# The second block's input projection on x times its weights, with the norm's factor applied at evacuation

## The reference

```
x = x + gate * (p @ ple_proj)            # end of block 1, gate = sigmoid(x @ ple_gate)
x = rms_norm(x, final_g)                 # factor 1 and gain final_g
a = rmsnorm(x, norm_pre_mix_2)           # factor 2 and gain norm_pre_mix_2
proj = a @ w_in_2                        # q,k | v | o gate | gates | c_q | c_kv | k_r
```

## Time and profile before

| | |
|---|---|
| median of 3 runs | 1454.25 us (1454.07 to 1454.81) |
| profiled execution | 1455.51 us, its span 1453.7 us |
| TensorE busy | 1367.2 us, 94% |
| DVE, ACT, POOL busy | 45%, 36%, 36% |
| mean granted TensorE clock | 0.967 |

### The profile page before, as it was taken

The page is one execution under the profiler, slowest core; times in us unless marked ns, Lnnn a source line. Parts: engine busy times, 40 slices in busy tenths (PEclk is TensorE's granted clock), DMA queues, the critical chain, the costliest instruction groups (busy, mean ns, idle before and its releaser), DMA issues.

```text
span 1453.7 us, 15764 instructions
## 1 busy us (share of the span) xinstructions
PE 1367.2 (94%) x6273; PEld 1087.5 (75%) x6273; DVE 652.8 (45%) x856; ACT 521.7 (36%) x794; POOL 519.0 (36%) x229
## 2 busy tenths in 40 slices
PE   4899989999999999999997999889979999999997
PEld 3677889868888888888884875556648888888885
DVE  6547866345422621121365624556465532514223
ACT  4567211254322221221343444444444322313232
POOL 2233250133444444444541432211214444444440
PEclk7899999999999999999998999999989999999998
DMA  5222210122333333332331322100113333333321
GB/s 167 59 61 70 58 30 15 44 73 87 109 96 93 101 98 92 100 99 84 107 96 35 87 66 51 44 29 30 44 44 87 94 95 102 98 91 101 99 75 58
DMA packets 211360, 111.66 MB, mean 77 GB/s; under 512 B 16140, under 2 KB 209496, under 8 KB 211288
## 3 DMA queue, kind: packets, MB, share of 16 engines
q1 hardware_dynamic: 210488, 109.81, 26.5%
q10 hardware_dynamic: 672, 0.79, 0.2%
q0 software_dynamic: 128, 0.07, 0.0%
HBM read 108.55 MB, written 2.10 MB: 76 GB/s over the span
## 4 chain that ended last, share of the span: by engine, by line
PE 86%; DVE 9%; ACT 3%; issue 1%; POOL 1%; DMA 0%; DVEq 0%; ACTq 0%; SPq 0%
PE bank L1711 22%; PE bank L1713 22%; PE bank L1712 21%; PE aux L1886 2%; PE aux L1899 1%; PE bank L1734 1%; PE aux L1061 1%; PE bank L1735 1%; PE bank L1736 1%; PE aux L1896 1%; PE bank L1046 1%; DVE al L2246 1%; DVE rstd L2254 1%; PE aux L975 1%; PE aux L987 1%
## 5 line engine op out<-in xcount | busy, mean ns | idle before, releaser
L1673 POOL TENSOR_TENSOR wl<-raw,wh 128x1024 fp32r<-128x1024 f32 (+1 forms) x202 | 496.6, 2460 | 870.8 <-ACT wh L1990 870.5
L1711 PE MATMUL bank<-ah,wh 128*128 128x512 f32 x984 | 391.7, 398 | 0.1
L1713 PE MATMUL bank<-al,wh 128*128 128x512 f32 x984 | 384.5, 391 | 0.0
L1712 PE MATMUL bank<-ah,wl 128*128 128x512 f32 x984 | 384.5, 391 | 0.0
L1990 ACT CAST wh<-raw 128x1024 fp32r<-128x1024 f32 (+1 forms) x202 | 209.2, 1039 | 352.5 <-PE bank L1713 338.2
L1711 PEld LDWEIGHTS bank<-ah,wh 128*128 128x128 f32 x984 | 185.6, 189 | 43.6 <-issue 5.5
L1712 PEld LDWEIGHTS bank<-ah,wl 128*128 128x128 f32 x984 | 185.7, 189 | 38.9 <-issue 1.4
L1713 PEld LDWEIGHTS bank<-al,wh 128*128 128x128 f32 x984 | 185.5, 188 | 39.1
L1711 PE MATMUL bank<-yh,wh 128*128 128x512 f32 x432 | 168.7, 391 | 0.0
L1713 PE MATMUL bank<-yl,wh 128*128 128x512 f32 x432 | 168.2, 389 | 0.0
L1712 PE MATMUL bank<-yh,wl 128*128 128x512 f32 x432 | 168.1, 389 | 0.0
(11 more groups left out here) (385 smaller groups left out, 1689.3 us busy)
## 6 DMA issues: line engine op xcount, KB each, us to landing
raw<-in_w_up SPq DMA_DIRECT2D x54, 512.0 KB, 4.0
raw<-in_w_down SPq DMA_DIRECT2D x48, 512.0 KB, 4.1
raw<-in_w_in SPq DMA_DIRECT2D x40, 512.0 KB, 3.9
raw<-in_w_gate SPq DMA_DIRECT2D x22, 512.0 KB, 3.8
raw<-in_w_out SPq DMA_DIRECT2D x16, 512.0 KB, 3.7
raw<-in_ple_gate SPq DMA_DIRECT2D x8, 512.0 KB, 4.0
raw<-in_w_down SPq DMA_DIRECT2D x8, 384.0 KB, 3.4
xtok<-in_x SPq DMA_DIRECT2D x4, 512.0 KB, 5.3
```

The costliest lines, as they stand in the source:

```text
L1673: nc.gpsimd.tensor_tensor(wl[b % SPLIT][:, 0:w], raw[b % RAW][:, 0:w], wh[b % SPLIT][:, 0:w].bitcast(F32), ALU.subtract).then_inc(wl_ready, 1)
L1711: nc.tensor.matmul(ps, h[:, c:c + P], mh[:, k, :], start=(n == 0), stop=False)
L1712: nc.tensor.matmul(ps, l[:, c:c + P], mh[:, k, :], start=False, stop=False)
L1713: last = nc.tensor.matmul(ps, h[:, c:c + P], ml[:, k, :], start=False, stop=(n == nk - 1))
```

## The change

- `pgate` reads `yh[1]`, `yl[1]` (free at that time) in place of `ah`, `al`; the splitting of x goes there.
- While the `pgate` tiles run, ACT fills `ah` with x · gains and DVE (`scaled_low`) fills `al`, for each k as soon as x k is final. `gains` is now computed before the loop.
- The last `pgate` tile is done whole. The sums over channels stand inside the pair `gates2`, `qk2` 0: `first_sums` behind k = 1, `last_sums` behind k = 5.
- The factor is kept as a row, `nrow` (the same 512 numbers on all partitions), and, for `v2`, where tokens lie on the partitions, as columns `ncol`, which four tiny products with one partition of `nrow` make after `qk2` 2.
- Every tile of the projection is multiplied by it when it is read. DVE becomes the reader of `qk2`, `o2`, `cq2` and `ckv2`; ACT then works from SBUF. `v2` stays with ACT, with `ncol` as scale.

The core of the diff:

```diff
-                  gate="act", up="dve", down="dve", proj="act", pgate="act", gates2="dve", qk2="act", v2="act",
-                  cq2="act", ckv2="act", o2="act", uq2="dve", uk2="act", uv2="dve", wouta="dve",
+                  gate="act", up="dve", down="dve", proj="act", pgate="act", gates2="dve", qk2="dve", v2="act",
+                  cq2="dve", ckv2="dve", o2="dve", uq2="dve", uk2="act", uv2="dve", wouta="dve",
...
-                    gemm("pgate", m, ready=(al_ready, KD * F_PLE) if m == 0 else None)
-            gemm("pgate", KD - 1, part=(0, 2))
-            ssq(2, early=True)
...
-            gemm("pgate", KD - 1, part=(1, 2))
-            ssq(2)
...
+                    gemm("pgate", m, mov=(yh[1], yl[1]), ready=(al_ready, KD * F_PLE) if m == 0 else None)
+            gemm("pgate", KD - 1, mov=(yh[1], yl[1]))
+            gemm_pair(("gates2", 0), ("qk2", 0), (al_ready, KD * F_NORM3), between={1: first_sums, 5: last_sums})
...
+                if k == 0:
+                    act.wait_ge(gains_ready, 1)
+                    act.wait_ge(gemm_done, LAST_USE[F_NORM2])
+                    act.wait_ge(al_ready, KD * F_NORM3)
+                nc.scalar.activation(ah[:, k, :], x[:, k, :], ACT.Copy, scale=gains[:, k:k + 1]).then_inc(ah_ready, 1)
...
-            link(nc.scalar.activation(sq[:, 0, :], sq[:, 0, :], ACT.Ln, bias=eps2[:, 0:1], scale=1.0 / D))
-            nc.scalar.activation(sq[:, 0, :], sq[:, 0, :], ACT.Exp, scale=-0.5).then_inc(rstd_ready, 1)
-            for k in range(KD):
-                upper(F_NORM3, k, k, h32[:, k % 3, :], (h32_ready, H32_BASE[F_NORM3] + k + 1))
+            link(nc.scalar.activation(nrow[:, :], sq[:, 0, :], ACT.Ln, bias=eps2[:, 0:1], scale=1.0 / D))
+            nc.scalar.activation(nrow[:, :], nrow[:, :], ACT.Exp, scale=-0.5).then_inc(rstd_ready, 1)
...
+            def scaled_low(k):
+                dve.wait_ge(ah_ready, KD * F_NORM3 + k + 1)
+                nc.vector.scalar_tensor_tensor(al[:, k, :], x[:, k, :], gains[:, k:k + 1], ah[:, k, :].bitcast(F32),
+                                               ALU.mult, ALU.subtract).then_inc(al_ready, 1)
...
+                if m > 0:
+                    scaled_low(m - 1)
             dve.wait_ge(x_gated, KD)
+            scaled_low(KD - 1)
...
-            for k in range(KD):
-                dve.wait_ge(al_ready, KD * F_NORM3 + max(0, k - 2))
-                nc.vector.scalar_tensor_tensor(h32[:, k % 3, :], x[:, k, :], gains[:, k:k + 1], both, ALU.mult,
-                                               ALU.mult).then_inc(h32_ready, 1)
-                if k > 0:
-                    lower(F_NORM3, k - 1, k - 1, h32[:, (k - 1) % 3, :])
...
             gemm("qk2", 1)
             gemm("qk2", 2)
+            pe.wait_ge(rstd_ready, 4)
+            for c in range(NC):
+                last = nc.tensor.matmul(aux[3][:, c:c + 1], nrow[0:1, c * P:(c + 1) * P], ones[0:1, 0:1], start=True,
+                                        stop=True)
+            last.then_inc(ncol_ps, 1)
             pe.wait_ge(forget_sums_ready, 1)
...
-                nc.scalar.copy(craw2[j % 2][:, 3:3 + T], bank[t % NBANK][:, :])
-                tile("qk2", j, lambda ps: nc.scalar.activation(cc2[j % 2][:, :], ps, ACT.Copy,
-                                                               scale=g_of("conv_w_2", 12 + j)))
+                tile("qk2", j)
+                evacuated(act, "qk2", j)
+                nc.scalar.activation(cc2[j % 2][:, :], craw2[j % 2][:, 3:3 + T], ACT.Copy,
+                                     scale=g_of("conv_w_2", 12 + j)).then_inc(last_tap, 1)
...
-                    tile("o2", j, lambda ps: nc.scalar.activation(o, ps, ACT.Exp, scale=-1.0))
+                    tile("o2", j)
                     evacuated(act, "o2", j)
+                    link(nc.scalar.activation(o, o, ACT.Exp, scale=-1.0))
...
+            def scaled_qk(j):
+                ps = tile("qk2", j)
+                if j >= 2:
+                    dve.wait_ge(conv2_done, j - 1)
+                    dve.wait_ge(last_tap, j - 1)
+                freed(nc.vector.tensor_tensor(craw2[j % 2][:, 3:3 + T], ps, nrow[:, :], ALU.mult))
...
+            dve.wait_ge(ncol_ps, 1)
+            nc.vector.tensor_copy(ncol[:, :], aux[3][:, 0:NC]).then_inc(ncol_ready, 1)
+            scaled_qk(1)
             conv(0)
+            scaled_qk(2)
             dve.wait_ge(cb_ps, 1)
...
+                elif kind == "proj2":
+                    if i == "o2":
+                        freed(nc.vector.tensor_tensor(og[:, s, :], tile("o2", s), nrow[:, :], ALU.mult))
+                    else:
+                        freed(nc.vector.tensor_tensor(cq[:, s if i == "cq2" else 2, :], tile(i, s), nrow[:, :], ALU.mult))
...
+                    if n in between:
+                        between[n]()
```

More of the change, by code:

```diff
@@ L247, in build @@
         rcol = sb("rcol", [P, NC])
+        ncol = sb("ncol", [P, NC])
         gains = sb("gains", [P, KD])
@@ L362, in build @@
         cq = sb("cq", [P, 3, T], at=offs["vt2"])
+        nrow = sb("nrow", [P, T], at=offs["vt2"] + 4 * 3 * T)
         pm = sb("pm", [P, 3, T], at=offs["trig"])
@@ L560, in build @@
         out_ready = signal("out_ready")
+        gains_ready = signal("gains_ready")
+        ncol_ps = signal("ncol_ps")
+        last_tap = signal("last_tap")
+        ncol_ready = signal("ncol_ready")
+        g2_scaled = signal("g2_scaled")
         SPLIT_AT = [2 * NC * (t + 1) + 1 for t in range(3)]
@@ L1178, in scalar_second @@
                 for c in range(NC):
-                    tile("v2", (pair, c), lambda ps: nc.scalar.copy(v2[:, c, pair * 256:(pair + 1) * 256],
-                                                                    ps[:, 0:256]))
+                    act.wait_ge(ncol_ready, 1)
+                    tile("v2", (pair, c), lambda ps: nc.scalar.activation(v2[:, c, pair * 256:(pair + 1) * 256],
+                                                                          ps[:, 0:256], ACT.Copy,
+                                                                          scale=ncol[:, c:c + 1]))
                     if pair == 1 and c == 0:
@@ L1214, in proj @@
                 else:
-                    tile(kind, j, lambda ps: nc.scalar.copy(cq[:, j if kind == "cq2" else 2, :], ps))
+                    tile(kind, j)
             def keys(j):
@@ L1419, in vector_second @@
             conv(2)
+            scaled_qk(3)
             conv(3)
@@ L1715, in gemm, with gemm_pair @@
                     last.then_inc(gemm_done, 1)
-            def gemm_pair(first, second, ready, order=None):
+            def gemm_pair(first, second, ready, order=None, between={}):
                 t = state["t"]
@@ L2035, in upper @@
                 act.wait_ge(*wait)
-                nc.scalar.copy(ah[:, k, :], src).then_inc(ah_ready, 1)
+                nc.scalar.copy((yh[1] if fill == F_PLE else ah)[:, k, :], src).then_inc(ah_ready, 1)
             tables(LN_EXP_TABLES)
```

52 lines of the change are left out of this document (29 added, 23 removed).

## The result

The changed kernel takes **1441.32 us** (median of 4 runs, 1440.84 to 1441.97), the kernel before 1454.53 us in the same comparison (1454.07 to 1456.53). The ratio is 0.9905, 95% interval 0.9892 to 0.9917: 13.2 us faster. The forecast was 1442.8.

The account below looks back on a forecast made before the run. TensorE, busy 94% of the span, was taken as the bound, gaining only where it waits or runs slowly. −16.5 + 2.1 + 2.0 + 0.9 = −11.5 gave a median of 1442.8 us; 8-in-10 range 1438.5 to 1447.8.

Parts of the forecast that it names:

- The stall: From pgate tile 7 to qk2 1: the pair no longer waits for the norm and al, −16.5 us.
- The `pgate` loop: One ACT copy and one DVE instruction more per pgate period just fit, so cost 0.
- rival 2: DVE misses its slot in the pgate loop, GpSimd holds the x add, first sums wait: 1445.5, chance 0.10.
- The factor: Behind the pair: nrow, gates2 reading and forget sums come later, tiny transposes take 0.6; cost 0 to 1 us.
- The conv chain: New DVE work delays c4 and the chain that releases TensorE, with a stall ahead of qk2 3: +2.1 us.
- The heads: Mixer heads: DVE reads o2 2 only behind latent_norms, so ACT and TensorE go on later: +2.0 us.
- The clock: Head 2's wait grows to 3.4 us and may bring a half-rate stretch; half its cost taken, +0.9 us.
- Rival 1: The later slips (c4 chain and heads) stay hidden behind other slack: 1439, chance 0.12.
- Rival 3: In-order reading costs everywhere in the heads, 6.9 us in place of 2.0: 1447.7, chance 0.15.
- Rival 5: Slower: GpSimd holds the products with nrow, so DVE bounds the projection: 1457.3, chance 0.04.
- Rival 4: The pair starts no earlier than its last operand, al 7, 5.8 us lost: 1448.6, chance 0.03.

Follow-up runs that it names:

- e3: Changed kernel with all six sums ahead of the pair and the pair held until the norm's factor is ready: 1446.42 us.
- e4: Changed kernel with the DVE operation scaled_low done twice per pgate tile, first into a scratch row: 1444.45 us.
- e9: Changed kernel with no tile multiplied by the factor (gates take a constant 0.25) and ACT reading qk2, o2, cq2, ckv2 as before: 1439.01 us.
- e2: Changed kernel with the four tiny products for ncol moved from behind qk2 2 to behind the first v tile: 1442.16 us.
- e10: e9 with GpSimd waiting for the forget sums before its two subtractions for v's weights: 1438.97 us.
- e13: Changed kernel with the edits of e1 and e2 and the GpSimd hold of e10 together, nothing left out: 1439.60 us.
- e8: Changed kernel with o2, cq2 and ckv2 left unscaled and read by ACT as before the change: 1440.61 us.
- e1: Changed kernel with DVE reading o2 2 behind the second latent tile, ahead of the last of the three: 1439.80 us.

## Why the prediction was right, step by step

**The stall, −16.5.** Measured −16.9. The six sums took 21.56 − 16.32 = 5.24 with their seams, and not the 5.5 allowed for, which is most of the difference. The slack for `al` 7 was there: its two making instructions took 3.52 from 768.28, so to 771.8 (forecast 772.8, wanted 780.7). The waits of before are gone and the clock is full. Of the 16.9, e3 prices what hangs on the factor alone at 3.4 us.

**The `pgate` loop, 0.** Right, with its margin: x add 0.25 us ahead of GpSimd, 0.26 in the earlier trace rows. e4 shows what lies beyond: rival 2 (1445.5) was a real one, its trigger one instruction away. Its path was another than written: the first sums did not wait, the weights' low part was late.

**The factor.** `gates2` read at +0.32 behind the pair's end (forecast +0.3), forget sums at +11.9 (forecast 10.0 to 12.4, the late end if two subtractions meet the scans: both did). The tiny products take 1.03 and not 0.6: the bound of one fp32 product (0.86) was too low for four.

**The conv chain, +2.1.** The size was near (+2.7) and c4's place right (+15.7, forecast 15.4 to 16.4); *what released TensorE was not what I wrote.* I had the DVE chain from c4 set v tile 4, with a stall ahead of `qk2` 3. In the changed kernel there is no such stall: between `qk2` 1 and v tile 4 the only wait is 0.57 us for the weights' low part. That part waits for ACT's casts, and these for its reading of the four v tiles. Before, ACT read all four without a pause, so the DVE chain ahead of it was the bound. Now it stops for the last one, and TensorE is. First before, then the changed kernel:

```profile
824.53 1.25 ACT L1179 COPY v<-bank 128x256 f32<-128x256 f32 x4
```

```profile
808.79 1.19 ACT L1200 ACTIVATE v<-bank,ncol 128x256 f32<-128x256 f32 x3
810.25 0.47 ACT L1200 ACTIVATE v<-bank,ncol 128x256 f32<-128x256 f32 x1 [0.28 <-PE bank L948]
```

By 0.28 us only: the two paths run nearly level. TensorE's own is +1.0 up to v tile 0 (tiny products and forget sums meet at 794.24; e9 and e2 show that the sums alone would do) and +1.5 by the half clock in v tile 0 (its 24 matmuls take 4.46 us, 2.97 before), which is absent before:

```profile
813.60:817.00 3.40, 3.40 (x29) 3.40 (x29) 3.19 (x4) 1.75 (x3) 1.58 (x1) 1.00 0.15 54
```

Without that half clock the predicted chain would be the bound, by an estimate from these rows some 0.3 us sooner: in e10 and e13, where the clock is full, ACT reads the four tiles without a pause and `qk2` 3 does start late (0.88 us of waiting in e10, 0.3 us in e13). So it was luck that the term came out near, a clock loss that I had looked for elsewhere having the size of the chain's slip; and the new DVE work is hidden behind it, not free: without it c4 comes 0.9 us sooner (+14.9 in e9).

**The heads, +2.0.** Measured +2.0, the wait 3.40 as forecast, and e8 and e1 confirm the cause: DVE's reading of the tiles, and of o2 2 above all.

**The clock, +0.9.** *Its sign was wrong.* The stretch that I had priced did come. The 3.40 us wait was followed by half clock (the 1.54 us one before the change was not), and 3 us of work at half rate are 1.5 lost:

```profile
900.00:903.00 3.00, 2.99 (x4) 1.17 (x4) 0.16 (x1) 0.00 (x1) 0.00 (x0) 0.50 0.03 5
```

But the length of the wait does not decide it: e3's wait of 3.16 us was followed by full clock, e1's of 1.85 by 6.6 us at half. And the part behind head 2 as a whole is 1.5 *shorter*. Its clock record, summed over windows of 1 us, has 30.4 us at half rate, this stretch included, against 37.4 before: of the stretches that stood 11 and 46 to 56 us behind that product in the profile of before, one of 3.3 us is left. The saved 7 us at half rate are worth 3.5 at most. I had counted only what I could see being added. With the 1.5 lost at v tile 0 the clock's whole balance is near nothing, and not +0.9. This is where most of the 1.5 us lies by which the forecast was too high: by the marks the terms were −16.9, +2.7, +2.0 and −1.5, together −13.7, against −16.5, +2.1, +2.0 and +0.9.

**Rivals.** Rival 1 (nothing slips, 1439) fails by the marks: +2.7 and +2.0 are there. Rival 3 (1447.7) fails: the heads cost 2.0 in all. Rival 5 fails: products of a bank with `nrow` take 0.67 to 0.69 wherever they stand, also beside GpSimd. Rival 4 fails: the pair starts without a wait, and `al` 7 is ready 9 us before it is wanted.

## What to carry to other kernels

A scale that belongs to a row can leave the critical path by being applied after the product, and the gain can be read in advance from one stretch of the timeline: useful matmuls against the stretch's length. When a DVE instruction is added beside GpSimd's subtractions, look at which of the two *begins* first in each period: one instruction more, with 0.25 us of margin, cost 1.4 us at the pair, and a longer stretch at half clock stood behind it. And before a chain of another engine is billed, ask whether TensorE's own list would be done sooner. Here the two were 0.28 us apart, and taking the DVE work away (e9) moved v tile 4 by 0.03 us.
